# Attention scores of a tuned two-block kernel: 64-row matmuls per head, or 128-row matmuls with zeroed queries

## The chip, the cores and the metric

The kernel runs on one core of a Trainium2 chip. The time is the device time of one execution in microseconds; the kernel before takes 2179.59 us as the median of three runs (2178.39 to 2180.96). Traces are of one profiled execution each.

## What is computed

Everything is float32 and works on 256 positions of width 2048. A first block (modulated RMS norm, a mixer of four kinds of attention, SwiGLU) is followed by a second one of two layers (projections, pooling or attention, memory attention, layer norm). The change touches the first mixer alone. Its heads all have the same core, cut here to one:

```
for every head h:                       # head size 64, 256 positions
    s = q[h] @ k[h].T * 64 ** -0.5 + bias[h]   # causal; bias: slopes, forgetting sums or a mask
    p = softmax(s, axis=-1)
    o[h] = p @ v[h]
```

There are 7 "fox" heads, 8 "nsa" heads (each with three attentions: chosen blocks, window, compressed keys), 9 "dil" heads and 4 "diff" heads with two maps of size 64 each.

## The kernel before

Each large product `x @ w` streams its weights from HBM in parts of 128 rows by up to 512 columns. SyncE loads two parts at a time into a ring of 8 slots (`raw`). ACT writes the rounded part `w_hi` (L420), DVE the rest `w_lo` (L467), and PE multiplies each part three times for each of two tiles of 128 positions (L536 to L538). A ring of four split parts (`HILO`) ties them together: ACT may split part n once PE has used part n-4. The same thing holds in all stages, and DVE also sums the modulation's weights (L446) between its parts.

The first mixer's attention is written between those parts. While the stages `win` and `wout` stream (208 parts), the heads are worked off in 25 pairs, called duos (class `Duo`, L677). The order is by hand: duo i has the number c = 13 + 6i of a part (`DUO_AT`, L881), and each engine does a step of the duo ahead of a part counted from c:

- PE: `turn` (L733, L735: queries and keys of both heads transposed into PSUM bank 4) ahead of part c-3; `scores` (L749) ahead of c; `turn_probs` (L761) ahead of c+10; `outputs` (L776) ahead of c+13.
- ACT: `early` (L785: bank 4 copied to `qkT`) ahead of its split c+2; `exps` (L794) c+10; `copy` (L802: transposed probabilities to `probsT`) c+15.
- DVE: `maxima` (L814) c+4, `stats` c+13, `normed` (L855 to L865) c+16. POOL writes the bias table `tab` (L1226) of a duo once the maxima of the one before are done.

So duos overlap: ahead of part c+3 of ACT's queue stands the `copy` of the duo two back. In `qkT` the 64 rows 0 to 63 hold the first head and rows 64 to 127 the second, queries and keys beside each other, in two buffers that alternate by duo. `scores` waits for the duo's `qkT`, for the maxima of the duo before (its PSUM banks 5 and 6) and for the `copy` of the duo two back, and then does, for each head on its 64 rows, one matmul of 128 columns (first 128 queries, 128 keys) and one of 256. A float32 matmul that is no transpose leaves two records in the trace.

The second mixer has pairs of heads of size 128 (class `Pair`, L885). From the fifth pair on, its `scores` (L934) are four float32 matmuls of 128, 256, 128 and 256 columns on all 128 rows.

Of the kernel before, what the change touches and what calls it, by code (L numbers as in the profile page):

```python
# [29 lines left out]
P = 128  # L30
T = 2
SEQ = P * T
# [3 lines left out]
HD = 64  # L36
# [171 lines left out]
def program(nc, x, c, ada_w, ada_b, norm_mix_g, norm_ffn_g, w_in, fox_f_bias, cmp_w1, cmp_w2, cmp_pos,  # L208
            diff_lambda, diff_subln_g, w_out, w_gate, w_up, w_down, final_g, mem, w_in2, w_out2,
            w_mem_kv, ln_g, ln_b, pool_w, pool_scale, w_kv, out):  # L210
    f32, f32r, i32 = mybir.dt.float32, mybir.dt.float32r, mybir.dt.int32
    ACT, ALU, AX = mybir.ActivationFunctionType, mybir.AluOpType, mybir.AxisListType
    ds = bass.ds
    ctx = ExitStack()
    with ctx:
# [7 lines left out]
        def at(name, shape, dt, off):  # L223
            size = 4 * int(np.prod(shape[1:]))
            assert off % 32 == 0 and off + size <= arena_bytes, (name, off, size)
            return nc.alloc_sbuf_tensor_at(name, shape, dt, offset=base + off)

        def new(name, shape, dt=f32):
            off = top[0]
            top[0] += (4 * int(np.prod(shape[1:])) + 31) // 32 * 32  # L230
            return at(name, shape, dt, off)

        def region(size):
            off = top[0]
            top[0] += size
            return off
# [33 lines left out]
        r_stg = region(20480)  # L270
# [5 lines left out]
        tab = at("tab", [P, 2, 384], f32, r_stg)  # L276
        probs = at("probs", [P, 2, 2, 384], f32, r_stg + 3072)
        probsT = at("probsT", [P, 2, 384], f32, r_stg + 9216)
        qkT = at("qkT", [P, 2, 2, SEQ], f32, r_stg + 12288)
        pair_qkT = at("pair_qkT", [P, 2, 2, SEQ], f32, r_stg + 16384)  # L280
        pair_probs = [at("pair_probs0", [P, 2, 512], f32, r_stg + 8192), at("pair_probs1", [P, 2, 512], f32, r_one + 57344)]
        pair_pT = [at("pair_pT0", [P, 2, 512], f32, r_stg + 12288), at("pair_pT1", [P, 2, 512], f32, r_one + 61440)]
# [2 lines left out]
        rows = new("rows", [P, 2, P])  # L285
# [38 lines left out]
        ps = ctx.enter_context(nc.psum_tensor("ps", [P, 8, 512], f32))  # L324

        def o3(ap, a):
            return ap.rearrange("p (a b) -> p a b", a=a)
# [4 lines left out]
        def S(name):  # L332
            if name not in sems:
                sems[name] = ctx.enter_context(nc.semaphore(name))
            return sems[name]
# [51 lines left out]
        def beside(work):  # L387

            ks = {k for _, k in work}
            return {k: (lambda p, j, k=k: work[j + 1, k]() if (j + 1, k) in work else None) for k in ks}  # L390
# [286 lines left out]
        class Duo:  # L677

            def __init__(self, i, kind, h0, projected, valued):

                self.i, self.kind, self.h0, self.par = i, kind, h0, i % 2
                self.projected, self.valued = projected, valued
                self.dv = 128 if kind == "diff" else HD
                self.nsa = kind in ("slc", "win", "cmp")
                self.x0 = {"fox": 0, "dil": 960, "diff": 1536}.get(kind, 448) + (128 if kind == "diff" else HD) * h0
# [49 lines left out]
            def scores(self, pe):  # L738
                pe.wait_ge(S("at_qkT"), self.i + 1)
                if self.i == 0:  # L740
                    pe.wait_ge(S("cmp_pos"), 1)
                if self.i:
                    pe.wait_ge(S("at_max"), self.i)
                if self.i >= 2:
                    pe.wait_ge(S("at_pT"), self.i - 1)
                for h in range(2):
                    q, k = (qkT[h * HD:(h + 1) * HD, self.par, kind, :] for kind in range(2))
                    for t, c0, nk in SPANS:
                        last = nc.tensor.matmul(ps[:, 5 + h, c0:c0 + nk], q[:, t * P:(t + 1) * P], k[:, 0:nk],  # L749
                                                start=True, stop=True)  # L750
                last.then_inc(S("at_scores"), 1)
# [28 lines left out]

            def early(self, act):
                act.wait_ge(S("at_turned"), self.i + 1)
                if self.i >= 2:
                    act.wait_ge(S("at_scores"), self.i - 1)
                act.activation(qkT[:, self.par, :, :], o3(ps[:, 4, :], 2), ACT.Copy).then_inc(S("at_qkT"), 1)  # L785

            def exps(self, act):
                act.wait_ge(S("at_max"), self.i + 1)
# [328 lines left out]
        def _(pool):  # L1117
            g = nc.gpsimd
            cn = [0]

            def chain(ins):
                cn[0] += 1
                ins.then_inc(S("pool_chain"), 1)
                pool.wait_ge(S("pool_chain"), cn[0])
# [21 lines left out]
                    last = g.iota(dist[:, kk, c0:c0 + n].bitcast(i32), [[-1, n]], base=q0 + 256, channel_multiplier=1)  # L1146
            chain(last)
            chain(g.memset(cmask[:, :], 0.0))
            for c0, n, q0 in spans:
                g.affine_select(out=dist[:, 0, c0:c0 + n], in_=dist[:, 0, c0:c0 + n], compare_op=ALU.is_ge, fill=MASKED,  # L1150
                                base=q0, pattern=[[-1, n]], channel_multiplier=1)
                g.affine_select(out=dist[:, 4, c0:c0 + n], in_=dist[:, 4, c0:c0 + n], compare_op=ALU.is_ge, fill=MASKED,
                                base=q0 - (CMP_LEN - 1), pattern=[[-CMP_STRIDE, n]], channel_multiplier=1)
                last = g.affine_select(out=cmask[:, c0:c0 + n], in_=cmask[:, c0:c0 + n], compare_op=ALU.is_ge,
                                       fill=-MASKED, base=q0, pattern=[[-1, n]], channel_multiplier=1)
# [698 lines left out]
        def _(dve):  # L1854
# [69 lines left out]
            def columns(of, first):  # L1924
                return lambda k: of[:, first + k:first + k + 1]
            _, low_u1 = mod_low_of(dve, "u1", actT, columns(gain[:, 0, :], 0), columns(modT, 0), lambda g: 7)

            def quarter_gains(q):
# [449 lines left out]
```

## Time and profile before

| | us |
|---|---|
| median of three runs | 2179.59 |
| profiled execution, device time | 2179.85 |
| its span from first to last instruction | 2178.1 |
| PE busy, share of the span | 2074.3 (95%) |
| DVE busy | 1435.7 (66%) |
| ACT busy | 1069.9 (49%) |
| POOL busy | 121.7 (6%) |
| share of PE in the chain that ended last | 82% |
| granted TensorE clock, mean | 0.986 |

Busy times overlap each other. A busy share says little by itself; the chain that ended last and the waits ahead of an instruction say which engine sets the time in a stretch. "PE" rows are matmuls and "PEld" rows are the loads of their stationary operand. A timeline row "0.93 ... x8" begins at its first number and covers eight instructions that follow each other; since matmuls are pipelined, a matmul of 0.39 us can follow the one before after 0.23.

### The profile page before, as it was taken

To read this page: it belongs to the slowest core of one execution; us is meant where nothing else is said; L and a number is where in the kernel's file an instruction comes from. 1 tells how busy PE (TensorE), PEld (TensorE's weight loads), DVE (VectorE), ACT (ScalarE), POOL (GpSimd) and SP (SyncE) were. 2 spreads that over 40 slices of the span, in tenths; PEclk is the share of its full clock that TensorE was granted. 3 is DMA by queue.
4 is the path that set the end of the run, shared out by engine and by line. 5 is a ranking of instruction groups with operands and counts; after the bars stand their busy time and mean duration, and the time that the engine had idled before them with its cause. 6 is when DMAs were issued, how large, how long until landed. Compare 5 with 4: busy or idle time off the path is not lost.

```text
span 2178.1 us, 28401 instructions
## 1 busy us (share of the span) xinstructions
PE 2074.3 (95%) x9850; PEld 1705.3 (78%) x9850; DVE 1435.7 (66%) x2485; ACT 1069.9 (49%) x1963; POOL 121.7 (6%) x188
## 2 busy tenths in 40 slices
PE   6997999998989999999999999999999899999996
PEld 5776787877767887888888888788788688888885
DVE  5987787778878777655556555854465655555556
ACT  3544555555435544445544454454454555555542
POOL 2000012114203000000000000000000000000000
PEclk9998999999999999999999999999999999999998
DMA  8998787776777887666565665574466455555562
GB/s 316 365 347 302 242 263 242 237 260 206 262 256 233 282 262 255 193 193 191 186 192 191 195 186 184 176 248 126 146 193 215 143 157 173 174 164 174 170 220 93
DMA packets 281468, 468.88 MB, mean 215 GB/s; under 512 B 17121, under 2 KB 111553, under 8 KB 279937
## 3 DMA queue, kind: packets, MB, share of 16 engines
q1 hardware_dynamic: 278576, 451.32, 64.3%
q0 software_dynamic: 2768, 15.98, 2.2%
q8 instruction: 71, 1.16, 0.2%
q14 instruction: 53, 0.43, 0.1%
HBM read 465.13 MB, written 2.10 MB: 215 GB/s over the span
## 4 chain that ended last, share of the span: by engine, by line
PE 82%; DVE 7%; issue 6%; DMA 2%; ACT 2%; SPq 0%; POOL 0%; DVEq 0%; POOLq 0%; ACTq 0%
PE ps L536 25%; PE ps L538 24%; PE ps L537 24%; DVE w_lo L467 2%; PE ps L776 1%; DVE acc_a L446 1%; DMA raw<-in_w_in 1%; PE ps L749 1%; PE ps L1588 1%; PE ps L956 1%; PE ps L934 1%; PE ps L761 1%; ACT w_hi L420 1%; DMA raw<-in_ada_w 1%; DMA X<-in_x 1%
## 5 line engine op out<-in xcount | busy, mean ns | idle before, releaser
L420 ACT ACTIVATE w_hi<-raw 128x512 fp32r<-128x512 f32 (+1 forms) x1328 | 831.9, 630 | 1023.5 <-PE ps L538 971.5
L467 DVE TENSOR_TENSOR w_lo<-raw,w_hi 128x512 fp32r<-128x512 f32 (+1 forms) x1328 | 906.5, 693 | 648.4 <-ACT w_hi L420 643.2
L536 PE MATMUL ps<-w_hi,actT 128*128 128x512 f32 (+2 forms) x1920 | 776.6, 404 | 17.4 <-DVE w_lo L467 11.7
L538 PE MATMUL ps<-w_hi,actT 128*128 128x512 f32 (+2 forms) x1920 | 750.2, 391 | 0.0
L537 PE MATMUL ps<-w_lo,actT 128*128 128x512 f32 (+2 forms) x1920 | 748.8, 390 | 0.0
L536 PEld LDWEIGHTS ps<-w_hi,actT 128*128 128x128 f32 x1920 | 363.5, 189 | 102.3 <-DVE w_lo L467 12.3
L538 PEld LDWEIGHTS ps<-w_hi,actT 128*128 128x128 f32 x1920 | 362.7, 189 | 77.1
L537 PEld LDWEIGHTS ps<-w_lo,actT 128*128 128x128 f32 x1920 | 364.3, 190 | 70.2 <-issue 1.7
L536 PE MATMUL ps<-w_hi,hidT 128*128 128x512 f32 x352 | 138.3, 393 | 3.0 <-DVE w_lo L467 3.0
L538 PE MATMUL ps<-w_hi,hidT 128*128 128x512 f32 x352 | 137.1, 390 | 0.0
L537 PE MATMUL ps<-w_lo,hidT 128*128 128x512 f32 x352 | 137.0, 389 | 0.0
L446 DVE SCALAR_TENSOR_TENSOR acc_a<-raw,c_col,acc_a 128x1024 f32<-128x1024 f32 x75 | 100.1, 1334 | 3.1 <-issue 2.6
L536 PE MATMUL ps<-w_hi,mixT 128*128 128x512 f32 x256 | 100.2, 391 | 1.5 <-DVE mixT L2262 1.5
L538 PE MATMUL ps<-w_hi,mixT 128*128 128x512 f32 x256 | 99.6, 389 | 0.0
L537 PE MATMUL ps<-w_lo,mixT 128*128 128x512 f32 x256 | 99.6, 389 | 0.0
L536 PEld LDWEIGHTS ps<-w_hi,hidT 128*128 128x128 f32 x352 | 66.1, 188 | 18.5 <-DVE w_lo L467 2.8
L538 PEld LDWEIGHTS ps<-w_hi,hidT 128*128 128x128 f32 x352 | 66.1, 188 | 14.0
L537 PEld LDWEIGHTS ps<-w_lo,hidT 128*128 128x128 f32 x352 | 66.1, 188 | 13.3
L536 PE MATMUL ps<-w_hi,memT 128*128 128x512 f32 x128 | 52.0, 407 | 11.7 <-DVE memT L600 8.5
L536 PEld LDWEIGHTS ps<-w_hi,mixT 128*128 128x128 f32 x256 | 48.1, 188 | 12.2 <-DVE mixT L2262 2.3
L538 PEld LDWEIGHTS ps<-w_hi,mixT 128*128 128x128 f32 x256 | 48.1, 188 | 10.1
L537 PEld LDWEIGHTS ps<-w_lo,mixT 128*128 128x128 f32 x256 | 48.1, 188 | 9.7
(287 smaller groups left out, 1609.5 us busy)
## 6 DMA issues: line engine op xcount, KB each, us to landing
raw<-in_w_in SPq DMA_DIRECT2D x208, 512.0 KB, 3.8
raw<-in_ada_w SPq DMA_DIRECT2D x192, 512.0 KB, 5.4
raw<-in_w_out SPq DMA_DIRECT2D x96, 512.0 KB, 4.2
raw<-in_ffn_w_gate SPq DMA_DIRECT2D x176, 256.0 KB, 2.9
raw<-in_ffn_w_up SPq DMA_DIRECT2D x176, 256.0 KB, 3.1
raw<-in_ffn_w_down SPq DMA_DIRECT2D x88, 512.0 KB, 3.9
raw<-in_w_kv_shared SPq DMA_DIRECT2D x48, 512.0 KB, 3.6
raw<-in_w_mem_kv SPq DMA_DIRECT2D x32, 512.0 KB, 6.8
```

Of the source, the lines that this page charges most:

```text
L420: act.activation(w_hi[:, g, 0:w], raw[:, slot_of(st, it), b, 0:w], ACT.Copy).then_inc(hi_ready, 1)
L446: ins = nc.vector.scalar_tensor_tensor(acc[:, :], both, c_col[:, it.ch:it.ch + 1], acc[:, :], ALU.mult, ALU.add)
L467: nc.vector.tensor_tensor(w_lo[:, g, 0:w], raw[:, slot, b, 0:w], w_hi[:, g, 0:w].bitcast(f32), ALU.subtract).then_inc(blocks_read, 1)
L536: nc.tensor.matmul(o, hi, w_hi[:, g, 0:w], start=first_k, stop=False)
L537: nc.tensor.matmul(o, hi, w_lo[:, g, 0:w], start=False, stop=False)
L538: last = nc.tensor.matmul(o, lo, w_hi[:, g, 0:w], start=False, stop=last_k)
L749: last = nc.tensor.matmul(ps[:, 5 + h, c0:c0 + nk], q[:, t * P:(t + 1) * P], k[:, 0:nk], start=True, stop=True)
L761: last = nc.tensor.transpose(ps[:, 5 + h, d:d + P], probs[:, self.par, h, c0 + kt * P:c0 + (kt + 1) * P], ident[:, :])
L776: last = nc.tensor.matmul(o, probsT[:, h, d:d + P], self.v(kt, h), start=(kt == 0), stop=(kt == nk // P - 1))
L934: last = nc.tensor.matmul(ps[:, 6 + h, c0:c0 + nk], pair_qkT[:, h, 0, t * P:(t + 1) * P], pair_qkT[:, h, 1, 0:nk], start=True, stop=True)
L956: last = nc.tensor.matmul(o, self.pT[:, h, d:d + P], self.v(kt, h), start=(kt == 0), stop=(kt == nk // P - 1))
L1588: last = nc.tensor.matmul(ps[:, 6 + t, 0:384], pool_block(grp * 3 + kk)[:, t * P:(t + 1) * P], poolw_s[:, grp, kk, :], start=(kk == 0), st ...
```

## The change

The scores contract over all 128 rows. `qkT` becomes three planes of 256 columns in one buffer: plane 0 holds the first head's queries in rows 0 to 63 and zeros below, plane 1 zeros above and the second head's queries in rows 64 to 127, plane 2 the keys of both heads. The zeros are written once, by a memset on POOL at the start. ACT's one copy of 128x512 becomes two of 64 partitions by 256 and one of 128x256. With a single buffer, the copy waits for the scores of the duo before (two before until now), and the first one for the zeros.

```diff
-        qkT = at("qkT", [P, 2, 2, SEQ], f32, r_stg + 12288)
+        qkT = at("qkT", [P, 3, SEQ], f32, r_stg + 12288)
...
                 for h in range(2):
-                    q, k = (qkT[h * HD:(h + 1) * HD, self.par, kind, :] for kind in range(2))
+                    q, k = qkT[:, h, :], qkT[:, 2, :]
                     for t, c0, nk in SPANS:
                         last = nc.tensor.matmul(ps[:, 5 + h, c0:c0 + nk], q[:, t * P:(t + 1) * P], k[:, 0:nk],
                                                 start=True, stop=True)
...
             def early(self, act):
                 act.wait_ge(S("at_turned"), self.i + 1)
-                if self.i >= 2:
-                    act.wait_ge(S("at_scores"), self.i - 1)
-                act.activation(qkT[:, self.par, :, :], o3(ps[:, 4, :], 2), ACT.Copy).then_inc(S("at_qkT"), 1)
+                if self.i:
+                    act.wait_ge(S("at_scores"), self.i)
+                else:
+                    act.wait_ge(S("q_zero"), 1)
+                for h in range(2):
+                    rows = slice(h * HD, (h + 1) * HD)
+                    act.activation(qkT[rows, h, :], ps[rows, 4, 0:SEQ], ACT.Copy)
+                act.activation(qkT[:, 2, :], ps[:, 4, SEQ:2 * SEQ], ACT.Copy).then_inc(S("at_qkT"), 1)
...
             chain(g.memset(cmask[:, :], 0.0))
+            g.memset(qkT[:, 0:2, :].rearrange("p h s -> p (h s)"), 0.0).then_inc(S("q_zero"), 1)
```

PE's order of matmuls and DVE's order stay as they are. ACT's queue around the copy of one duo, between the splits of two parts (L794 are the exponentials of the duo before, L802 the `copy` of the duo two back), before:

```order
L420 ACTIVATE w_hi<-raw 128x512 [waits parts_used,w_loaded0]
L785 ACTIVATE qkT<-ps 128x512 [waits at_scores,at_turned]
L420 ACTIVATE w_hi<-raw 128x512 [waits parts_used]
L802 ACTIVATE probsT<-ps 128x768 [waits at_pv,at_ptr]
L420 ACTIVATE w_hi<-raw 128x512 [waits parts_used,w_loaded2]
L794 ACTIVATE probs,sm<-probs,sm 128x128 [waits at_rs,at_max]
```

and with the change (lines below L681 of the file have moved down by one, those behind `early` by six, those behind the memset by seven):

```order
L420 ACTIVATE w_hi<-raw 128x512 [waits parts_used,w_loaded0]
L790 ACTIVATE qkT<-ps 64x256 [waits at_scores,at_turned]
L790 ACTIVATE qkT<-ps 64x256
L791 ACTIVATE qkT<-ps 128x256
L420 ACTIVATE w_hi<-raw 128x512 [waits parts_used]
L808 ACTIVATE probsT<-ps 128x768 [waits at_pv,at_ptr]
L420 ACTIVATE w_hi<-raw 128x512 [waits parts_used,w_loaded2]
L800 ACTIVATE probs,sm<-probs,sm 128x128 [waits at_rs,at_max]
```

Nothing changes places: two copies come in at the place of the one, ahead of the same split and the same `copy`.

## Rows read from the trace of the kernel before

**Rows 1.** The page: the chain that ended last, by engine
```profile
PE 82%; DVE 7%; issue 6%; DMA 2%; ACT 2%; SPq 0%; POOL 0%; DVEq 0%; POOLq 0%; ACTq 0%
```

**Rows 2.** Stretches: length, each engine's busy time (instructions), clock, DMA share, GB/s
```profile
246.00:300.00 54.00, 53.60 (x318) 42.83 (x317) 45.70 (x116) 32.80 (x76) 8.34 (x8) 1.00 0.77 249
...
500.00:563.00 63.00, 50.42 (x309) 42.32 (x310) 56.15 (x129) 31.43 (x82) 33.85 (x33) 0.97 0.68 221
```

**Rows 3.** Groups by shape, whole span: busy us, mean ns, idle before
```profile
L749 PE MATMUL ps<-qkT 64*128 64x256 f32 x100 | 15.7, 377 | 0.0
L934 PE MATMUL ps<-pair_qkT 128*128 128x256 f32 x56 | 14.7, 379 | 0.0
```

**Rows 4.** Timeline of PE and PEld at duo 2 (start, us, ...)
```profile
271.62 0.39 PE L538 MATMUL ps<-w_hi,actT 128*128 128x512 f32 x1
272.11 0.56 PEld L749 LDWEIGHTS ps<-qkT 64*128 64x128 f32 x8 [0.53 <-issue]
272.14 0.93 PE L749 MATMUL ps<-qkT 64*128 64x128 f32 x8
...
273.00 0.19 PEld L536 LDWEIGHTS ps<-w_hi,actT 128*128 128x128 f32 x1 [0.33 <-issue]
...
273.33 0.39 PE L537 MATMUL ps<-w_lo,actT 128*128 128x512 f32 x1
```

**Rows 5.** The same of PE at duo 1
```profile
261.18 0.39 PE L538 MATMUL ps<-w_hi,actT 128*128 128x512 f32 x1
261.49 0.93 PE L749 MATMUL ps<-qkT 64*128 64x128 f32 x8
...
262.69 0.39 PE L537 MATMUL ps<-w_lo,actT 128*128 128x512 f32 x1
```

**Rows 6.** Timeline of ACT at duo 2, then a group of ACT by shape
```profile
269.21 0.58 ACT L785 ACTIVATE qkT<-ps 128x512 f32<-128x512 f32 x1
...
270.66 0.63 ACT L420 ACTIVATE w_hi<-raw 128x512 fp32r<-128x512 f32 x1 [0.87 <-PE ps L538]
...
271.20 0.79 ACT L802 ACTIVATE probsT<-ps 128x768 f32<-128x768 f32 x1
...
L1731 ACT ACTIVATE cumk<-ps 128x256 f32<-128x256 f32 x1 | 0.4, 365 | 0.0
```

**Rows 7.** Chain that ended last, 246 to 532 us (start, us, what)
```profile
308.90 0.80 ACT probsT L802
309.83 0.93 PE ps L749 x8
...
488.26 0.93 PE ps L749 x8
```

**Rows 8.** Timeline of PE at the second mixer's pair 4
```profile
1836.50 0.39 PE L538 MATMUL ps<-w_hi,actT 128*128 128x512 f32 x1
1836.73 1.47 PE L934 MATMUL ps<-pair_qkT 128*128 128x128 f32 x8
...
1838.27 0.39 PE L537 MATMUL ps<-w_lo,actT 128*128 128x512 f32 x1
```

**Rows 9.** Chain that ended last, behind 490 us
```profile
510.11 1.23 DVE acc_a L446
```

**Rows 10.** Timeline at duo 22
```profile
526.92 0.60 ACT L785 ACTIVATE qkT<-ps 128x512 f32<-128x512 f32 x1
...
529.37 0.93 PE L749 MATMUL ps<-qkT 64*128 64x128 f32 x8 [1.71 <-ACT probsT L802]
```

**Rows 11.** Timeline of POOL, start of the program
```profile
10.52 0.53 POOL L1162 MEMSET upper<- 128x512 f32 x1
...
38.77 0.73 POOL L1176 DMA_DIRECT2D X<-in_x  x1 [26.07 <-PE ps L569]
```

**Rows 12.** Stretches around the half clock, columns as in rows 2
```profile
522.80:526.20 3.40, 3.40 (x16) 3.36 (x15) 2.11 (x4) 0.63 (x1) 3.30 (x5) 0.50 0.84 273
...
563.70:567.10 3.40, 3.40 (x10) 2.61 (x9) 1.11 (x3) 1.12 (x2) 0.00 (x0) 0.51 0.82 246
```

## The prediction, made before the changed kernel had run

> **What bounds the kernel now.** I begin with the page's chain of waits that ended last: it runs through PE for 82% of the span [rows 1]. Whatever sits in PE's queue between two steps of the weight stream is therefore paid in full, unless PE has to wait there for somebody else. The mixer's 25 duos lie between 250 and 560 us; the table of stretches shows PE busy 53.6 of 54 us at their start, but only 50.4 of 63 us from 500 us on, where DVE is busy 56.2 of 63 [rows 2]. So the stage has two parts with different limits.
>
> To price the change, a mean duration is of no use: a score matmul on 64 rows takes 377 ns, and the second mixer's score matmul with the same 256 columns on 128 rows takes 379 ns [rows 3]. Matmuls are pipelined, so what counts is from which start to which start PE's queue advances. Each float32 score matmul leaves two records, so a duo's four matmuls are the "x8" of the rows. Two kinds of place exist in the kernel before:
>
> - A duo whose scores wait. L538 starts at 271.62, the scores at 272.14, the L536 behind them at 273.00 and the L537 at 273.33 [rows 4]. Undisturbed steps are 0.23 us apart. The weight loader stands idle 0.53 us before the scores and 0.33 us behind them.
> - A duo whose scores don't wait: L538 261.18, scores 261.49, L537 262.69 [rows 5]. Here too the first score starts 0.31 us after the L538, not 0.23.
>
> What the waiting ones wait for is seen from ACT: the copy of the transposed probabilities of the duo two back (L802) runs from 271.20 to 271.99, right ahead of 272.14 [rows 6], and in the chain of the duo at 309.83 that copy is the link in front of the scores [rows 7]. Of the 25 groups of L749 in the timeline, 7 start 0.23 to 0.32 us behind the matmul before them (numbers 0, 1, 10, 12, 13, 21, 24, counted from 0), and 18 start 0.49 us or more behind it.
>
> **The price of 128 rows.** The trace has the changed operation almost exactly: the second mixer's pairs 4 to 9 do four float32 score matmuls on 128 rows with 128, 256, 128 and 256 columns. There L538 starts at 1836.50, the scores at 1836.73 and the second matmul behind them at 1838.27 [rows 8]. The eight matmuls cover 1.47 us there and 0.93 in a duo [rows 4, 8]. So:
>
> - first score to second matmul behind: 1.54 us with 128 rows, 273.33 - 272.14 = 1.19 us with 64. **+0.35 us** for a duo that waits, since its start is set by ACT's copy and does not move.
> - preceding L538 to second matmul behind: 1838.27 - 1836.50 = 1.77 against 262.69 - 261.18 = 1.51. **+0.26 us** for a duo that does not wait; the 0.09 between the two is what it gets back at the entrance.
>
> The 64-row matmuls of the kernel before thus run overlapped: their eight records pass in about half the time, and the holes in front and behind cost less than that saves. The Trainium skill says both things, in "TensorEngine Tiling (Array Packing)", section Key Properties: tiles of the array load and multiply in parallel, and a change of the tiling mode drains the engine. Its drain speaks for this change and its parallel tiles against it; by the drain alone the sum would be a gain of 7.3 us, which is rival 1 below.
>
> **Where it lies on the path.** In the chain, PE stands at the scores of each of the duos 0 to 19 (the last at 488.26 us), with the copy as a link in front for some [rows 7]. For these 20: 5 that don't wait at 0.26 = 1.30 and 15 that wait at 0.35 = 5.25. Behind 490 us the chain goes over to DVE: beside duo 21 (scores at 510.83) it is DVE's acc_a [rows 9], and beside duos 20, 23 and 24 DVE's splits and sums do the same; DVE's list does not grow, so a longer PE there is taken out of PE's own waits. I cost duos 20, 21, 23 and 24 at nothing; if that cover is not there they cost 2 x 0.35 + 2 x 0.26 = 1.2 us. Duo 22 is on the chain again (529.37) [rows 10]: +0.35.
>
> **ACT's three copies.** L785 takes 0.58 us for 128x512. The new form is two copies of 64 partitions x 256 and one of 128x256. A 128x256 copy out of PSUM is a row of its own, 365 ns; L420 runs from 270.66 to 271.29 and the next instruction starts at 271.20, so ACT overlaps neighbours by 0.09 [rows 6]. 64 partitions have no row for this; between nothing saved against 128 partitions (0.365) and half of it (0.18), I take the first, since it is the dearer one; it matters at a single duo, as follows. That makes 3 x 0.365 - 2 x 0.09 = 0.92, +0.33 us a duo. Behind the copy ACT stands idle 0.87 us until PE has used a part (L420 at 270.66) [rows 6]: the 0.33 disappears in it, and the probabilities' copy that the scores wait for keeps its time. The exception is duo 22: ACT works without a hole from its copy at 526.92 to the probabilities' copy that PE waits 1.71 us for [rows 10]: +0.33 on the path.
>
> **The rest.** The new wait, for the scores of the duo before instead of two before, costs nothing. If a duo's scores stand ahead of part c, its copy stands in ACT's queue behind the split of part c+1; that split has waited until PE had used part c-3, and the scores of the duo before stand ahead of part c-6. This had to be looked at, since the splits that DVE and then PE live on are queued behind that wait. The zeroing on POOL is one memset of 128x512, 0.53 us by the row of `upper`, and POOL idles 26 us before its next appointment at 38.77 [rows 11]: nothing. No row tells zeros from other numbers on PE; I take them as alike.
>
> **Sum:** 1.30 + 5.25 + 0.35 + 0.33 = **+7.2 us**. The profiled execution took 2179.85 us (span 2178.1), 0.26 above the median 2179.59; on the median the forecast is 2179.6 + 7.2 = **2186.8 us**.
>
> **Rivals.**
> 1. *The holes were the cost (not slower).* At the eight new records: if they advanced at the pace of the eight old ones (0.56 us of loads) with no hole before or behind, each of the 21 duos on the path would save up to 0.33, and the five unwaited ones 0.08 more: 6.9 + 0.4 = 7.3, so 2172.3 us. The point from which it decides is 1.19 us from the first score to the second matmul behind; anything shorter is a gain. For it: the holes of 0.33 are real [rows 4]. Against it: the same form at 128 rows needs 1.54 [rows 8]. 5 in 100. This is what the drain in the Trainium skill's "TensorEngine Tiling (Array Packing)", Key Properties, would make of the change if the parallel tiles counted for nothing.
> 2. *The clock gives it back (no measurable change).* From 522.8 to 526.2 PE runs at 0.50 of full speed, and from 563.7 to 567.1 at 0.51 [rows 12], behind waits for DVE. Each such stretch does 1.7 us less work. A PE that is busier near the waits could lose both: 7.2 - 3.4 = +3.8, 2183.4 us. For it: the first of them lies on PE's part of the chain. Against it: the waits for DVE ahead of them stay, and the full clock before 500 us cannot rise. 12 in 100.
> 3. *ACT is late everywhere.* If the idle 0.87 is not there for the longer copy (or the 64-partition copies cost far more than their columns), the scores of every duo move by 0.33, where so far only duo 22 is charged: 24 x 0.33 = 7.9 on top, 2194.7 us. Against it: the hole is over twice the addition in nearly every duo. 7 in 100.
>
> **How the numbers follow.** The forecast has 76 in 100. That is less than the range must hold, so it reaches down to rival 2: 2183.4, less the 1.2 by which the lowest run lies under the median, is 2182.2. Upwards it takes in the 1.2 of the four covered duos, one more stretch at half clock (1.7) and the 1.4 by which the highest run lies above: 2191.1. What this kernel's measurement can tell from no change is 0.2%, 4.4 us. Slower by more: forecast and rival 3, 83 in 100. Within it: rival 2, 12. Faster: rival 1, 5.
>
> **What would show it.** In the changed profile the score records should step 0.11 and 0.22 us, the span of the "x8" grow from 0.93 to about 1.47 us, and the 0.33 us hole of the loader behind the scores be gone; the wait for L802's copy should stay at the same distance from the L538 ahead; ACT's idle ahead of L420 should shrink from 0.87 to about 0.54. PE's busy time from 246 to 500 us should lengthen the stretch by some 6.5 us, and the stretch behind it by less than 1.5. I am wrong if the distance from the first score to the second matmul behind is not near 1.54 us, or if it is and the duos come no further apart: from duo 5 to duo 19 it is 488.26 - 309.83 = 178.4 us now [rows 7], and should be 183.1 (three unwaited and eleven waiting ones).

## The result, and the profile after

The changed kernel takes 2190.56 us as the median of five runs (2188.71 to 2194.66); the kernel before took 2179.59, as the median of five (2175.84 to 2182.04), the three runs named at the start and two more. The ratio is 1.0052, with a 95% interval of 1.0041 to 1.0063: slower by 8.9 to 13.7 us, and by 11.0 from median to median. The forecast was +7.2, with a range up to +11.5. The profiled execution took 2188.71 us.

The page of the changed kernel, its head, its busy times and its chain by engine:

```profile
span 2187.0 us, 28454 instructions
...
PE 2084.9 (95%) x9850; PEld 1723.4 (79%) x9850; DVE 1435.8 (66%) x2485; ACT 1081.4 (49%) x2013; POOL 122.0 (6%) x189
...
PE 82%; DVE 7%; issue 6%; DMA 2%; ACT 2%; SPq 0%; POOL 0%; DVEq 0%; POOLq 0%; ACTq 0%
```

The chain's shares are those of [rows 1]. PE is busy 10.6 us longer, ACT 11.5 us, DVE as long as before. The span grew by 8.9 us, PE's busy time by more: what was added is time in which PE works and no wait. (Part of it is PE working at half clock; more on that below.)

The timeline of the changed kernel at duo 2, first PE and PEld, then ACT (start, length, engine, line, tiles; in brackets the idle time ahead and what ended it):

```profile
270.80 0.39 PE L538 MATMUL ps<-w_hi,actT 128*128 128x512 f32 x1
271.29 1.18 PEld L750 LDWEIGHTS ps<-qkT 128*128 128x128 f32 x8 [0.52 <-issue]
271.32 1.55 PE L750 MATMUL ps<-qkT 128*128 128x128 f32 x8
272.49 0.19 PEld L536 LDWEIGHTS ps<-w_hi,actT 128*128 128x128 f32 x1
272.94 0.40 PE L537 MATMUL ps<-w_lo,actT 128*128 128x512 f32 x1
...
268.39 0.76 ACT L790 ACTIVATE qkT<-ps 64x256 f32<-64x256 f32 x2
269.16 0.39 ACT L791 ACTIVATE qkT<-ps 128x256 f32<-128x256 f32 x1
269.85 0.63 ACT L420 ACTIVATE w_hi<-raw 128x512 fp32r<-128x512 f32 x1 [0.30 <-PE ps L538]
270.38 0.79 ACT L808 ACTIVATE probsT<-ps 128x768 f32<-128x768 f32 x1
```

Against [rows 4], the scores still start 0.52 us behind the L538 ahead of them, because they still wait for ACT's copy of the probabilities (L808, 270.38 + 0.79 = 271.17). The hole of 0.33 us in the loader behind them is gone. From the first score to the second matmul behind it is 272.94 - 271.32 = 1.62 us, where it was 1.19. On ACT the three copies take 269.16 + 0.39 - 268.39 = 1.16 us, where one took 0.58 [rows 6], and the idle time ahead of L420 went from 0.87 to 0.30.

Duo 1, whose scores don't wait (PE, same columns):

```profile
260.10 0.39 PE L538 MATMUL ps<-w_hi,actT 128*128 128x512 f32 x1
260.33 1.47 PE L750 MATMUL ps<-qkT 128*128 128x128 f32 x8
261.87 0.39 PE L537 MATMUL ps<-w_lo,actT 128*128 128x512 f32 x1
```

Here the first score follows after 0.23 us instead of the 0.31 of [rows 5], and from L538 to the second matmul behind it is 1.77 us instead of 1.51.

**Where the 11 us came in.** For this I lay the starts of each duo's scores beside each other. The chain of the changed kernel that ended last has duos 5 and 19:

```profile
310.31 1.55 PE ps L750 x8
...
494.10 1.55 PE ps L750 x8
```

They are 183.8 us apart, where they were 178.4 [rows 7]. The same reading for all kernels of this study, in us; "waits under 0.34" are those of the duos 0 to 19 whose first score starts less than that behind the matmul ahead of it:

| kernel | duo 0 to 19 | duo 19 to 24 | waits under 0.34 |
|---|---|---|---|
| before | 237.29 | 67.92 | 5 |
| changed | 244.55 | 69.82 | 5 |
| e1_three_copies | 237.28 | 68.53 | 5 |
| e2_rows_only | 245.99 | 69.33 | 5 |
| e3_same_rows | 249.06 | 70.76 | 5 |
| e6_heads_inside | 237.23 | 66.36 | 5 |
| e4_copy_sooner | 232.30 | 66.60 | 19 |
| e5_128_sooner | 236.97 | 66.53 | 20 |

Where the last but one column differs by more than the scores explain, it is by stretches at half clock: between duos 19 and 24 the kernel before, the changed one, e1, e2 and e4 have a whole one, e3 two, e5 and e6 none. In the changed kernel and in e2 a second one begins ahead of duo 24 and takes in its scores.

The change costs 7.26 us up to the start of duo 19's scores, 0.42 for that duo's own, and another 1.48 up to duo 24. Duo 24's own scores cost 1.28 more (they are below). That is 10.4 us in the mixer. Behind it, the starts of the weight matmuls of the two kernels keep their distance to within 0.25 us to the end of the program. The span grew by less, 8.9 us, because duo 0 starts earlier in this trace of the changed kernel, at 249.55 instead of 250.97 us. Over the eight traces that start spreads from 249.6 to 255.8 us, so only distances from duo 0 on are compared here.

Two further places in the timeline of the changed kernel, ACT at duo 22, then PE around duo 24:

```profile
533.20 0.76 ACT L790 ACTIVATE qkT<-ps 64x256 f32<-64x256 f32 x2
533.98 0.38 ACT L791 ACTIVATE qkT<-ps 128x256 f32<-128x256 f32 x1
534.25 0.59 ACT L1755 ACTIVATE actT<-ps 128x512 fp32r<-128x512 f32 x1
534.73 0.63 ACT L420 ACTIVATE w_hi<-raw 128x512 fp32r<-128x512 f32 x1
535.25 0.81 ACT L808 ACTIVATE probsT<-ps 128x768 f32<-128x768 f32 x1
...
561.86 0.47 PE L536 MATMUL ps<-w_hi,actT 128*128 128x512 f32 x1 [0.17 <-DVE w_lo L467]
...
562.64 0.63 PE L536 MATMUL ps<-w_hi,actT 128*128 128x512 f32 x1
...
563.92 2.49 PE L750 MATMUL ps<-qkT 128*128 128x128 f32 x8
566.06 0.58 PE L536 MATMUL ps<-w_hi,actT 128*128 128x512 f32 x1
```

PE at the same place in the kernel before:

```profile
554.63 0.47 PE L536 MATMUL ps<-w_hi,actT 128*128 128x512 f32 x1 [0.17 <-DVE w_lo L467]
...
556.18 0.93 PE L749 MATMUL ps<-qkT 64*128 64x128 f32 x8
557.04 0.50 PE L536 MATMUL ps<-w_hi,actT 128*128 128x512 f32 x1
```

The stretches of the changed kernel around duo 24 and a little behind it, columns as in [rows 2]:

```profile
562.60:566.00 3.40, 3.40 (x11) 2.85 (x10) 3.40 (x5) 1.78 (x7) 3.19 (x3) 0.50 0.56 169
572.80:576.20 3.40, 3.40 (x10) 2.63 (x9) 1.27 (x2) 1.12 (x2) 0.00 (x0) 0.51 0.75 242
```

At duo 22 ACT has no hole, so the longer copies move the probabilities' copy and with it the scores: they start 2.70 us behind the matmul ahead instead of 2.10. At duo 24 the scores fell into a stretch with a granted clock of 0.50 of full speed, which is the lower level of 1.2 GHz. From the first score to the L536 behind it is 566.06 - 563.92 = 2.14 us there, and was 557.04 - 556.18 = 0.86. The stretch had begun at 562.6, so the matmuls ahead of the scores were late too: from the first L536 shown to the first score it is 2.06 us instead of 1.55.

### The profile page after: what moved, and what is told of

The parts are those of the page before. It is cut to its first block, busy times and chain, and to the rows that moved or that the text cites. A ratio compares the mean times of both kernels' runs of the same rounds, so it can differ in the third digit from the quotient of the medians.

```text
span 2187.0 us, 28454 instructions
## 1 busy us (share of the span) xinstructions
PE 2084.9 (95%) x9850; PEld 1723.4 (79%) x9850; DVE 1435.8 (66%) x2485; ACT 1081.4 (49%) x2013; POOL 122.0 (6%) x189
## 3 DMA queue, kind: packets, MB, share of 16 engines
q8 instruction: 71, 1.16, 0.2%
## 4 chain that ended last, share of the span: by engine, by line
PE 82%; DVE 7%; issue 6%; DMA 2%; ACT 2%; SPq 0%; POOL 0%; DVEq 0%; POOLq 0%; ACTq 0%
PE ps L536 24%; PE ps L538 24%; PE ps L537 24%; DVE w_lo L467 2%; PE ps L750 2%; PE ps L777 1%; DVE acc_a L446 1%; DMA raw<-in_w_in 1%; PE ps L1595 1%; PE ps L962 1%; PE ps L940 1%; PE ps L762 1%; ACT w_hi L420 1%; DMA raw<-in_ada_w 1%; DMA raw<-in_w_mem_kv 0%
## 5 line engine op out<-in xcount | busy, mean ns | idle before, releaser
L420 ACT ACTIVATE w_hi<-raw 128x512 fp32r<-128x512 f32 (+1 forms) x1328 | 829.7, 629 | 1020.5 <-PE ps L538 968.7
L536 PE MATMUL ps<-w_hi,actT 128*128 128x512 f32 (+2 forms) x1920 | 778.5, 405 | 17.0 <-DVE w_lo L467 11.3
L538 PE MATMUL ps<-w_hi,actT 128*128 128x512 f32 (+2 forms) x1920 | 750.5, 391 | 0.0
L536 PEld LDWEIGHTS ps<-w_hi,actT 128*128 128x128 f32 x1920 | 363.7, 189 | 94.6 <-DVE actT L650 11.4
L538 PEld LDWEIGHTS ps<-w_hi,actT 128*128 128x128 f32 x1920 | 363.3, 189 | 77.1
L536 PE MATMUL ps<-w_hi,hidT 128*128 128x512 f32 x352 | 138.3, 393 | 3.0 <-DVE w_lo L467 3.0
L538 PE MATMUL ps<-w_hi,hidT 128*128 128x512 f32 x352 | 137.1, 389 | 0.0
L536 PE MATMUL ps<-w_hi,mixT 128*128 128x512 f32 x256 | 100.2, 391 | 1.5 <-DVE mixT L2269 1.5
L538 PE MATMUL ps<-w_hi,mixT 128*128 128x512 f32 x256 | 99.6, 389 | 0.0
L536 PEld LDWEIGHTS ps<-w_hi,hidT 128*128 128x128 f32 x352 | 66.1, 188 | 18.6 <-DVE w_lo L467 2.8
L538 PEld LDWEIGHTS ps<-w_hi,hidT 128*128 128x128 f32 x352 | 66.1, 188 | 13.9
L536 PE MATMUL ps<-w_hi,memT 128*128 128x512 f32 x128 | 51.7, 404 | 11.1 <-DVE memT L600 8.4
L536 PEld LDWEIGHTS ps<-w_hi,mixT 128*128 128x128 f32 x256 | 48.0, 188 | 12.1 <-DVE mixT L2269 2.3
L538 PEld LDWEIGHTS ps<-w_hi,mixT 128*128 128x128 f32 x256 | 48.1, 188 | 10.1
```

The costliest lines, as they stand in the source:

```text
L420: act.activation(w_hi[:, g, 0:w], raw[:, slot_of(st, it), b, 0:w], ACT.Copy).then_inc(hi_ready, 1)
L536: nc.tensor.matmul(o, hi, w_hi[:, g, 0:w], start=first_k, stop=False)
L538: last = nc.tensor.matmul(o, lo, w_hi[:, g, 0:w], start=False, stop=last_k)
```

## The experiments

Three things could carry the loss: the matmuls' rows, the three copies on ACT, and the single buffer. The first three kernels separate the rows from the other two, which e1 keeps together; the last three ask whether order or waits could win something.

### e1: three copies and one buffer, but 64 rows

Of the changed kernel, only the matmuls go back to 64 rows; planes, zeros and copies stay.

```diff
-                    q, k = qkT[:, h, :], qkT[:, 2, :]
+                    q, k = qkT[h * HD:(h + 1) * HD, h, :], qkT[h * HD:(h + 1) * HD, 2, :]
```

> The changed kernel with its three copies and its single buffer, but with scores on 64 rows each again (zeros unused, same result). Theory (the 128-row matmuls cost the time, ACT's copies only do at duo 22, where they stand on the path): the step from first score to second matmul behind is 1.19 us as before, ACT's copies still take 1.15 us, and the kernel is at 2179.6 + 0.6 to 1.5, so 2180.2 to 2181.1 us. Rival (ACT's longer copy or the single buffer carries the loss): 25 x 0.3 to 0.57 us, 2187 to 2191 us.

Measured: 2181.99 us (median of 10 runs) beside 2179.08 of the kernel before, ratio 1.0015 [1.0005, 1.0025]. Timeline at duo 2, ACT's first split behind the copies and PE:

```profile
271.90 0.63 ACT L420 ACTIVATE w_hi<-raw 128x512 fp32r<-128x512 f32 x1 [0.30 <-PE ps L538]
...
273.38 0.93 PE L750 MATMUL ps<-qkT 64*128 64x128 f32 x8
274.58 0.39 PE L537 MATMUL ps<-w_lo,actT 128*128 128x512 f32 x1
```

ACT looks as in the changed kernel (idle 0.30) and PE as before (1.20 us). From duo 0 to duo 19 nothing is lost (237.28 against 237.29 us), from 19 to 24 0.61 us, and that is the later copy at duo 22. So the copies and the single buffer cost 0.6 us in the trace. The median says +2.9, above what was expected, with an interval that begins at 1.1 (1.0005). The runs without a trace give a hint: the mean granted clock is 0.981 or 0.982 in six of the ten runs of e1, and in one of the twenty beside it. One stretch of 3.4 us at half clock lowers that mean by 3.4 x 0.5 / 2180 = 0.0008, so by this estimate these six had about two or three more of them than most runs of the kernel before. Whether the copies bring such stretches stays open.

### e2: 128 rows without zeros or new copies

Of the kernel before, only the rows change. Left out is the separation of the heads: without zeros, each score is the sum over both heads.

```diff
-                    q, k = (qkT[h * HD:(h + 1) * HD, self.par, kind, :] for kind in range(2))
+                    q, k = (qkT[:, self.par, kind, :] for kind in range(2))
```

> The kernel before with its one copy and two buffers, but each score matmul on all 128 rows without the zeros, so that each head's scores are the sum over both heads: the separation of the heads is left out. Theory: PE's part of the loss alone, 15 x 0.42 + 5 x 0.25 = 7.6 us for duos 0 to 19 and 1 to 3 us behind them, 2188 to 2190.5 us. Rival (the copies carry it): 2179.6 to 2182 us.

Measured: 2187.92 us (median of 5 runs), ratio 1.0044 [1.0027, 1.006], at the lower end of what was expected and 8.8 us over the kernel before. Timeline at duo 2, ACT and PE:

```profile
271.84 0.63 ACT L420 ACTIVATE w_hi<-raw 128x512 fp32r<-128x512 f32 x1 [0.87 <-PE ps L538]
...
272.79 0.39 PE L538 MATMUL ps<-w_hi,actT 128*128 128x512 f32 x1
273.31 1.55 PE L749 MATMUL ps<-qkT 128*128 128x128 f32 x8
274.93 0.40 PE L537 MATMUL ps<-w_lo,actT 128*128 128x512 f32 x1
```

ACT is as before (0.87) and PE as in the changed kernel (274.93 - 273.31 = 1.62 us). From duo 0 to 19 it lost 8.7 us: the same 7.3, and 1.4 in a stretch at half clock at 449 us that the changed kernel doesn't have. Up to duo 19 the rows alone carry the loss, and by the medians they carry 8.8 of the 11.0 us (5.9 to 13.1 by the interval); the rest is about what e1 has on top. That zeros cost PE what other numbers cost is seen here too: 1.62 us with and without them.

### e3: 64 rows, but both heads on the same ones

Here the second head's matmuls read rows 0 to 63 as the first's do, so the second head is left out of the scores. The number of rows is as before; what is taken away is that the heads lie on different rows.

```diff
-                    q, k = (qkT[h * HD:(h + 1) * HD, self.par, kind, :] for kind in range(2))
+                    q, k = (qkT[0:HD, self.par, kind, :] for kind in range(2))
```

> The kernel before, 64-row matmuls, but both heads read rows 0 to 63, so that the second head's scores are the first's: the second head of each duo is left out of the result. Theory (matmuls of the first head, rows 0 to 63, and of the second, rows 64 to 127, run at the same time): with one half of the array alone they follow each other, eight records need about 1.3 us as on 128 rows, the holes of 0.1 and 0.3 stay, and the distance from the first score to the second matmul behind is 1.6 to 1.9 us: 20 x 0.4 to 0.7 more, 2188 to 2194 us. Rival (half the rows make a float32 matmul cheaper by itself, whichever rows): nothing changes, 1.19 us and 2179.6 us.

Measured: 2198.28 us as the median of 2192.75 to 2200.78, ratio 1.009 [1.0073, 1.0107]: above what was expected. The profiled execution, with a span of 2191.0 us, is at the lower end of that. What the others had on top of it no trace shows; their granted clock was lower, 0.981 to 0.983 against 0.986. Timeline of PE and PEld at duo 2:

```profile
271.93 0.39 PE L538 MATMUL ps<-w_hi,actT 128*128 128x512 f32 x1
272.42 1.17 PEld L749 LDWEIGHTS ps<-qkT 64*128 64x128 f32 x8 [0.53 <-issue]
272.45 1.55 PE L749 MATMUL ps<-qkT 64*128 64x128 f32 x8
273.92 0.19 PEld L536 LDWEIGHTS ps<-w_hi,actT 128*128 128x128 f32 x1 [0.33 <-issue]
274.26 0.40 PE L537 MATMUL ps<-w_lo,actT 128*128 128x512 f32 x1
```

The eight matmuls on 64 rows now cover 1.55 us, exactly what eight on 128 rows cover, and the hole of 0.33 behind them is back: 274.26 - 272.45 = 1.81 us from the first score to the second matmul behind. Rows 0 to 63 alone take as long as all 128; the 0.93 us of the kernel before [rows 4] come from the heads lying on different rows. Both parts of the trade are now priced one by one, for a duo that waits: overlap saves 1.81 - 1.19 = 0.62 us, and the shape's change costs 1.81 - 1.62 = 0.19 us. Taken together they are the 0.43 of the change.

The Trainium skill, "TensorEngine Tiling (Array Packing)", Key Properties, says that different tiles can load and multiply in parallel and that a change of the tiling mode drains the engine. The trace agrees with both, and gives each its size here: 0.62 us against 0.19.

### e6: the two heads alternate

If the overlap comes from neighbours in the queue on different rows, an order h0, h1, h0, h1 could overlap more than h0, h0, h1, h1.

```diff
-                for h in range(2):
-                    q, k = (qkT[h * HD:(h + 1) * HD, self.par, kind, :] for kind in range(2))
-                    for t, c0, nk in SPANS:
+                for t, c0, nk in SPANS:
+                    for h in range(2):
+                        q, k = (qkT[h * HD:(h + 1) * HD, self.par, kind, :] for kind in range(2))
```

> The kernel before with the loops of scores exchanged: for each block of queries both heads, so 128, 128, 256, 256 columns with the rows changing each time (same result). Theory (the two heads' matmuls overlap): equal lengths stand beside each other and the last 256 columns are not alone, the distance from first score to second matmul behind falls from 1.19 to about 1.0 us and the kernel to 2179.6 - 2 to 4 us, 2175.5 to 2177.6 us. Rival (the overlap is not between heads): no change, 2179.6 us.

Measured: 2179.61 us, ratio 1.0 [0.999, 1.001]: a miss. Timeline of PE at duo 2:

```profile
276.50 0.39 PE L538 MATMUL ps<-w_hi,actT 128*128 128x512 f32 x1
277.03 0.93 PE L749 MATMUL ps<-qkT 64*128 64x128 f32 x8
278.22 0.39 PE L537 MATMUL ps<-w_lo,actT 128*128 128x512 f32 x1
```

The same 0.93 and 1.19 us. Sorted by start, the records of the kernel before already stand in pairs, 14 ns apart in duos that don't wait (steps 13, 200, 14, 98, 13, 205, 14 ns). By their shapes they are four of 64x128 and then four of 64x256, in both kernels, although the program before puts the first head's 256 columns ahead of the second head's 128. PE thus started the second head's matmuls beside the first's by itself, and the order of four matmuls in the program decides nothing.

### e4: the probabilities' copy one part sooner

In 15 of the duos 0 to 19 PE waits for ACT's copy of the transposed probabilities. The copy's own input is ready by c+14, so it can go one split earlier. Of the kernel before:

```diff
-                    elif n == c + 15:
+                    elif n == c + 14:
                         duo.copy(act)
```

> The kernel before (64-row scores, one copy) with ACT's copy of the transposed probabilities one split earlier, ahead of part c+14 instead of c+15, into the idle time ahead of that split. Theory (the scores of 18 duos wait for that copy, behind a split that itself waits for PE): the scores start 0.32 us behind the L538 ahead instead of 0.52, and 0.32 instead of 1.5 at the two duos where two proj copies stand in between; 13 x 0.2 + 2 x 1.2 + up to 1.5 at duo 22, so 4.5 to 6.5 us less, 2173 to 2175 us. Rival (ACT's early copy pushes the split of part c+14 and DVE's behind it, or the wait moves to another semaphore): less than 1.5 us gained, 2178 us or more.

Measured: 2175.58 us (11 runs) beside 2179.83, ratio 0.9979 [0.997, 0.9988]: faster than both kernels, by 4.3 us than the kernel before, a little less than expected. Timeline at duo 3, ACT and PE:

```profile
284.99 0.81 ACT L802 ACTIVATE probsT<-ps 128x768 f32<-128x768 f32 x1
285.70 0.60 ACT L785 ACTIVATE qkT<-ps 128x512 f32<-128x512 f32 x1
286.38 0.64 ACT L420 ACTIVATE w_hi<-raw 128x512 fp32r<-128x512 f32 x1
...
287.34 0.39 PE L538 MATMUL ps<-w_hi,actT 128*128 128x512 f32 x1
287.66 0.93 PE L749 MATMUL ps<-qkT 64*128 64x128 f32 x8
288.86 0.39 PE L537 MATMUL ps<-w_lo,actT 128*128 128x512 f32 x1
```

The copy now stands ahead of the duo's own. Of the first 20 duos, 19 have scores that start within 0.34 us, and waits of 1.5 us at duos 9 and 17 vanished too. Duo 0 to 19 takes 5.0 us less. The wait that the change left in place was worth about 4 us; PE is busy throughout the 254 us from 246 to 500, by the table of stretches of this kernel:

```profile
246.00:500.00 254.00, 254.00 (x1475) 209.22 (x1474) 203.20 (x530) 146.62 (x346) 39.36 (x37) 0.99 0.77 248
```

### e5: 128 rows with the sooner copy

The changed kernel with the same edit: does the dearer form lose less, once no duo waits?

> The changed kernel (128-row scores, three copies) with the same earlier copy of the probabilities. Theory: without the wait the first load of a score is hidden again (first step 0.11 instead of 0.18 us) and the start falls from 0.52 to 0.23 us behind the L538: 13 x 0.37 + 2 x 1.35 and up to 1.5 more at duo 22 less than the changed kernel, 7 to 9 us, so 2181.5 to 2183.5 us; against the 64-row kernel with the same copy it is dearer by 20 to 25 x 0.25, 5 to 6 us. Rival (three copies of 1.15 us and the 0.79 us of the probabilities no longer fit ACT's idle time, 1.45 us behind the start of the first): the split behind them starts 0.4 us later in each duo and the gain is under 3 us, 2187 us or more.

Measured: 2180.88 us (11 runs), ratio to before 1.0004 [0.9995, 1.0013]; 9.7 us under the changed kernel's median, 5.3 above e4's, and 0.6 below the range expected. Timeline at duo 3, ACT, PE and PEld:

```profile
287.84 0.39 ACT L791 ACTIVATE qkT<-ps 128x256 f32<-128x256 f32 x1
288.12 0.63 ACT L420 ACTIVATE w_hi<-raw 128x512 fp32r<-128x512 f32 x1
...
288.71 0.39 PE L538 MATMUL ps<-w_hi,actT 128*128 128x512 f32 x1
288.71 1.29 PEld L750 LDWEIGHTS ps<-qkT 128*128 128x128 f32 x8
288.94 1.47 PE L750 MATMUL ps<-qkT 128*128 128x128 f32 x8
290.48 0.39 PE L537 MATMUL ps<-w_lo,actT 128*128 128x512 f32 x1
```

All 20 duos look like pair 4 of the second mixer [rows 8], within 0.02 us: 0.23 us to the first score, 1.47 us of scores, 1.54 to the second matmul behind. Against e4, duo 0 to 19 takes 4.67 us more, 0.25 per duo, which is the price of the unwaited duo. So 64 rows are the better form in either setting.

## Why the prediction was right, and where its sizes were off

**Overlap against holes: right.** Its central step, that the 64-row matmuls of the two heads overlap and that this outweighs the holes, is what e2 and e3 show. Rival 1 asked for less than 1.19 us from the first score to the second matmul behind; 1.52 to 1.62 were measured up to duo 19.

**Unwaited duos: exact.** Forecast 1.54 and 1.77 us, +0.26 each. Measured 1.54 and 1.77, and 0.25 per duo between e4 and e5.

**Waiting duos: 0.42, not 0.35.** The step that was off is the transfer of pair 4's 1.54 us to duos that wait. Pair 4 doesn't wait: its first load starts 0.22 us ahead of its first matmul, and its second together with it. In a waiting duo the loader stood idle for 0.52 us, the first load starts 0.03 us ahead of the first matmul, the second 0.08 behind it, and the single records show the second matmul 0.18 us behind the first instead of 0.11. e5 shows that the wait is the cause: the same matmuls without it are back at 0.11 and 1.54. 15 duos at 0.07 make 1.05 us. The prediction had counted the waiting duo's entrance as free on both sides; its start is fixed, but what follows is not.

**ACT's three copies: hidden where the prediction said, but dearer.** +0.57 us instead of +0.33. The size of one was right (0.36 to 0.39 us, 64 partitions as much as 128), but the overlap of 0.09 between neighbours is missing: the copies start 0.37 and 0.40 us apart. The 0.87 of idle time was enough for it, with 0.30 left; e1 shows that it costs nothing up to duo 19, against rival 3. At duo 22 it cost 0.60 instead of 0.33.

**Duos 20, 21 and 23 at nothing: right. Duo 24 at nothing: wrong.** To see this, the starts of the same weight matmuls are laid beside each other in both traces. Duo 20 pushed them back by 0.41 us, and by the L536 at 506.56 us (512.80 in the changed kernel) 0.43 had come back in waits. Duo 21 pushed nothing back. Duo 23 took 0.25, and 0.27 had come back by the L536 at 554.63 (561.86). Duo 22 is the 0.60 + 0.42 above. What is left ahead of duo 24's scores, 0.5 us, came in behind that last L536, where the half clock begins, and the scores themselves took 1.28 more: 1.8 us for a term that was 0 in the sum and 0.26 in its bound. Some 0.25 of it is the form, by e5's price of an unwaited duo; the other 1.5 is the clock (an estimate from these figures).

**The clock: the other way round from rival 2.** The stretches at half clock of [rows 12] did not go away. They lie at 528.5 and 572.8 in the changed kernel: the L536 that starts at 563.91 us in the kernel before, in its second stretch, starts at 572.76 in the changed one. The one at 562.6, which holds duo 24's scores, is additional. e2's trace has it too, at 565.3 with duo 24 at 566.90; e1's and e5's have none at their duo 24. Three of e2's five runs have a mean clock of 0.986 or 0.987, as high as the best of the kernel before, so 128 rows don't always bring it. What does stays open: no run here was made for that.

**The sum.** Forecast 5.25 + 1.30 + 0.35 + 0.33 = 7.2 us. Measured in the trace 7.7 up to and with duo 19, where 6.55 stood, and 2.8 behind, where 0.68 stood: 10.4. The medians say 11.0. Of the 3.2 that were missing, 1.1 are the later second load behind a wait, 0.3 the copies at duo 22 and 0.1 its scores, and 1.8 duo 24, nearly all of it the half clock; duos 20, 21 and 23 add nothing. The stretch up to 500 us was to grow by some 6.5 us and the one behind by less than 1.5; the second was passed. The median 2190.56 lies 0.5 us below the upper end of the range: the sum alone was a third too small, and the range held because it had room for one more stretch at half clock.

## What to carry to other kernels

Small matmuls on different rows of PE can cost little more than those on one half alone (the eight records of both heads cover 0.93 us; in e3 the first four, one head's, cover 0.89); zeros that fill the rows give that up, and pay only where the holes of the change of shape are dearer than the overlap saves (here 0.19 us against 0.62). A cost read from instructions that follow their neighbours without a wait was too low behind a wait (1.54 against 1.62 us), where the second load came later. And before a matmul is reshaped, look at what it waits for: one copy moved one place up in ACT's queue won 4.3 us, where the new shape lost 11.

## What the runs showed of the hardware

- Matmuls of two heads, on rows 0 to 63 and 64 to 127, run in pairs whatever their order within the group of four (e6: 1.0 [0.999, 1.001]). In the kernel before, the second head's matmuls of 128 columns start 14 ns behind the first head's, ahead of the first head's 256 columns, which the program has before them.
- The same matmuls, all on rows 0 to 63, take as long as on 128 rows: 1.55 us for eight (e3, e2).
- The change of shape costs more where nothing waits. At duo 1 it is 2.16 us from L538 to the second matmul behind in e3, and 1.77 in the changed kernel, so 0.39, against 0.19 at a duo that waits: there, 0.09 at the entrance and 0.10 at the first load lie in the wait.
- ACT's neighbouring instructions overlap by 0.09 us in [rows 6]; copies of 64, 64 and 128 partitions of 256 columns, each 0.36 to 0.39 us, don't overlap each other, while the instruction behind the last of them does again at duo 22 (0.11 us).
- At a granted clock of 0.50 the weight matmuls start 0.43 us apart (562.6 to 563.9 in the changed kernel), at the full clock 0.23.
